# Output projections in split float32r by column halves with loads behind each half, and the first expert's rows selected from X by TensorE

## The reference, cut to what matters

```python
h = mixer_ab(x, ...)                 # layer 0: retention heads and pooling; mixed @ w_out at its end
h = mixer_c(x, ...)                  # layer 1: sparse attention; o @ w_out at its end
x = layer_norm(ALPHA * x + h, ln1_g[i], ln1_b[i])
m = hierarchical_moe(x, ...)         # top group, top 2 of its 8 experts; each expert:
                                     #   a, b = split(xt[tok] @ w_gu[e]); (silu(a) * b) @ w_down[e]
x = layer_norm(ALPHA * x + m, ln2_g[i], ln2_b[i])
x = x + sigmoid(x @ ple_w_gate[i]) * (p[i] @ ple_w_proj[i])
```

## Time and profile before

| | us |
|---|---|
| median of 3 runs | 1652.06 (1650.83 to 1652.81) |
| the profiled execution | 1653.78 |
| its span, first to last instruction | 1651.9 |
| mean granted TensorE clock | 0.957 |

### The profile page before, as it was taken

One profiled execution on the slowest core, in us unless ns is written; L12 is line 12 of the kernel. 1 busy time (PEld: TensorE's weight loads), 2 busy tenths in 40 slices (PEclk: granted clock), 3 DMA queues, 4 the chain that ended last, 5 costly groups with the idle time before them and its releaser, 6 DMA issues. The chain is left out here.

```text
span 1651.9 us, 17175 instructions
## 1 busy us (share of the span) xinstructions
PE 1441.9 (87%) x6216; PEld 684.8 (41%) x6216; DVE 410.2 (25%) x1020; ACT 314.9 (19%) x642; POOL 207.5 (13%) x327
## 2 busy tenths in 40 slices
PE   6998998998887789879998988989987888889887
PEld 5885463332222233224444456853322323333243
DVE  3424351000000001044068354330000000101172
ACT  3212011111011101012234574111101101101121
POOL 0000001211111111100000253011211111111100
PEclk9999989999999999999999999979999999999989
DMA  7107358999999999994200003299999999999840
GB/s 284 51 26 267 139 193 335 411 426 429 430 429 428 430 429 428 424 371 170 109 1 1 1 2 115 83 426 424 427 431 428 429 429 429 428 429 428 358 171 38
DMA packets 78306, 482.57 MB, mean 292 GB/s; under 512 B 18400, under 2 KB 20452, under 8 KB 45480
## 3 DMA queue, kind: packets, MB, share of 16 engines
q1 hardware_dynamic: 65800, 463.76, 67.5%
q0 software_dynamic: 10240, 16.82, 2.7%
q10 hardware_dynamic: 2208, 1.20, 0.2%
HBM read 474.91 MB, written 23.59 MB: 302 GB/s over the span
## 5 line engine op out<-in xcount | busy, mean ns | idle before, releaser
L910 PE MATMUL PS<-wide,w 128*64 128x512 f32 x1984 | 448.3, 601 | 49.4 <-ACT w L929 29.0
L924 PE MATMUL PS<-slim,w 128*64 128x512 f32 x992 | 252.8, 655 | 78.4 <-issue 77.0
L910 PEld LDWEIGHTS PS<-wide,w 128*64 128x64 f32 x1984 | 136.4, 138 | 329.4 <-issue 255.2
L924 PEld LDWEIGHTS PS<-slim,w 128*64 128x64 f32 x992 | 84.2, 149 | 241.2 <-issue 239.1
L936 DVE TENSOR_TENSOR w<-w,PS 128x256 f32<-128x256 f32 x64 | 27.0, 422 | 543.8 <-ACT w L933 543.8
L933 ACT ACTIVATE w<-PS 128x256 f32<-128x256 f32 x64 | 24.5, 383 | 501.8 <-PE PS L910 501.8
L1174 PE MATMUL PS<-wide,XT 128*128 128x512 f32 x256 | 117.8, 617 | 2.3 <-ACT XT L176 2.3
L1485 ACT ACTIVATE w<-PS,w 128x512 f32<-128x512 f32 x62 | 42.6, 687 | 313.2 <-PE PS L924 313.2
L939 DVE COPY w<-PS 128x256 f32<-128x256 f32 x64 | 27.2, 425 | 297.9 <-PE PS L917 297.9
L1352 POOL COPY w<-w 128x1 uint32 (+1 forms) x62 | 11.2, 181 | 660.3 <-ACT w L1485 660.3
L883 POOL DMA_INDIRECT w<-x_rows,w x64 | 67.2, 1050 | 72.3 <-POOL w L1345 51.6
(11 more groups left out here) (232 smaller groups left out, 1627.8 us busy)
## 6 DMA issues: line engine op xcount, KB each, us to landing
wide<-in_moe_w_gu SPq DMA_DIRECT2D x124, 2048.0 KB, 25.8
slim<-in_moe_w_down SPq DMA_DIRECT2D x62, 2048.0 KB, 25.7
w<-in_moe_w_gu SPq DMA_DIRECT2D x4, 2048.0 KB, 12.2
wide<-in_ple_w_gate SPq DMA_DIRECT2D x4, 2048.0 KB, 14.2
w<-in_ab_w_in SPq DMA_DIRECT2D x2, 2048.0 KB, 14.0
w_in<-in_ab_w_in SPq DMA_DIRECT2D x2, 2048.0 KB, 7.5
x_rows<-X SPq DMA_DIRECT2D x8, 512.0 KB, 2.6
XT<-in_moe_w_down SPq DMA_DIRECT2D x2, 2048.0 KB, 29.1
```

Source lines behind the costliest of these rows:

```text
L910: m = pe.matmul(PS[u * SLOTS:(u + 1) * SLOTS, 2 + q, :], xeT[q][:, k, :], gu[k].rearrange("p (a u c) -> p a u c", a=2, u=2)[:, :, u, :], s ...
L924: m = pe.matmul(PS[u * SLOTS:(u + 1) * SLOTS, 6 + q, :], gT[:, k, :], dn[k][:, u * NB:(u + 1) * NB], start=(k == 0), stop=(k == FF // P - 1))
```

## The change

1. Layer 0's output weights and mix are split too, and its 64 float32 products become 192 in float32r. The weights' raw halves are loaded during the input projection, once its sixteenth job is done. The first half is split there by ACT and DVE, the second in the retention stage by ACT and POOL. For each row of the mix ACT writes MT_HIGH and MT_RAW from bank 7 and POOL subtracts; for the last row DVE does it from PSUM.
2. `out_projection` goes over the column halves outside and the tiles inside, in both layers; layer 1's output weights are laid out by halves.
3. SP's loads stand in three places: before the sums (`load_first`), after the first column half (`load_half_way`), and after the last sum (`load_after_products`), this one ahead of the last tile's store to x_rows. In layer 0, expert 0 isn't loaded in the retention stage any more.
4. Expert 0's rows aren't gathered: DVE makes a selection matrix FIRST from the ranks, and TensorE multiplies X with it (`place_first`), before GP. The gather of expert 1 is alone. The filler products after GP are gone.

The diff, cut to its core:

```diff
+            OUT_RAW = [three(again(f"out_raw{c}", of, 0, 4096, F32)[:, :], NB) for c, of in enumerate(("w_high1", "w_low1"))]
+            OUT_LOW = [three(again(f"out_low{c}", of, 0, 4096)[:, :], NB) for c, of in enumerate(("w_high1", "w_low1"))]
+            OUT_HIGH = [three(again(f"out_high{c}", of, 0, 4096)[:, :], NB) for c, of in enumerate(("w_in0", "x_high"))]
+            MT_RAW = three(again("mixed0_raw", "w_low0", 0, 4096, F32)[:, :], SEQ)
+            MT_LOW = three(again("mixed0_low", "w_low0", 0, 4096)[:, :], SEQ)
+            MT_HIGH = three(again("mixed0_high", "x_low", 0, 4096)[:, :], SEQ)
...
+                    pj.wait_full(sp, 15)
+                    for c in range(2):
+                        sp.dma_start(OUT_RAW[c], rows(A["ab_w_out"][0, :, c * NB:(c + 1) * NB], NB))\
+                          .then_inc(s_wout[c], 16)
...
+                        if j in (16, 17):
+                            act.wait_ge(s_wl, len(PIECES))
+                            act.wait_ge(s_wout[0], 16)
+                            for k in range(4 * (j - 16), 4 * (j - 15)):
+                                act.activation(OUT_HIGH[0][:, k, :], OUT_RAW[0][:, k, :], ACT.Copy).then_inc(s_oh, 1)
...
+                    for k in range(KD):
+                        dve.wait_ge(s_oh, k + 1)
+                        dve.tensor_tensor(OUT_LOW[0][:, k, :], OUT_RAW[0][:, k, :], OUT_HIGH[0][:, k, :].bitcast(F32),
+                                          ALU.subtract).then_inc(s_ol, 1)
+                    dve.wait_ge(s_ol, KD)
...
-                sp.dma_start(w_out0[0], rows(A["ab_w_out"][0, :, 0:NB], NB)).then_inc(s_wout[0], 16)
-                sp.dma_start(w_out0[1], rows(A["ab_w_out"][0, :, NB:D], NB)).then_inc(s_wout[1], 16)
-                load_gu(sp, 0, 0, 0)
-                load_dn(sp, 0, 0, 0)
...
+                j = len(LAST) - 1
+                k = row_of(j)
+                dve.wait_ge(s_mh, j + 1)
+                dve.scalar_tensor_tensor(MT_LOW[:, k, :], PS[:, 7, :], gains[:, k:k + 1], MT_HIGH[:, k, :].bitcast(F32),
+                                         ALU.mult, ALU.subtract).then_inc(mt.sem_of(j), 1)
+                mt.wait_emptied(dve, j)
...
+            def _(pool):
+                for k in range(KD):
+                    pool.wait_ge(s_oh1, k + 1)
+                    pool.tensor_tensor(OUT_LOW[1][:, k, :], OUT_RAW[1][:, k, :], OUT_HIGH[1][:, k, :].bitcast(F32),
+                                       ALU.subtract).then_inc(s_ol1, 1)
+                for j in range(len(LAST) - 1):
+                    k = row_of(j)
+                    mt.wait_emptied(pool, j)
+                    pool.tensor_tensor(MT_LOW[:, k, :], MT_RAW[:, k, :], MT_HIGH[:, k, :].bitcast(F32), ALU.subtract)\
+                        .then_inc(s_ml, 1)
...
+                act.wait_ge(s_wout[1], 16)
+                for k in range(KD):
+                    act.activation(OUT_HIGH[1][:, k, :], OUT_RAW[1][:, k, :], ACT.Copy).then_inc(s_oh1, 1)
                 for j, (kind, i) in enumerate(LAST):
                     mt.wait_full(act, j)
-                    k = i if kind == "turn" else 4 + i
-                    act.activation(MT[:, k, :], PS[:, 7, :], ACT.Copy, scale=gains[:, k:k + 1])\
-                       .then_inc(mt.sem_of(j), 1)
...
-                    for t in range(T):
-                        for c in range(2):
+                    for c in range(2):
+                        for t in range(T):
                             pairs = products(t, c)
                             for r, (lhsT, rhs) in enumerate(pairs):
                                 m = pe.matmul(PS[:, 2 * t + c, :], lhsT, rhs, start=(r == 0),
                                               stop=(r == len(pairs) - 1))
                             m.then_inc(sums.full, 1)
-                            if t >= 2 and c == 0:
+                            if c == 1 and t >= 2:
                                 if t == 2:
                                     pe.wait_ge(s_wr, 64)
                                 logits(t - 2)
-                        if t >= 1:
-                            pe.wait_ge(norm.done, t)
-                            turn.pe(pe, t - 1)
+                            if c == 1 and t >= 1:
+                                pe.wait_ge(norm.done, t)
+                                turn.pe(pe, t - 1)
...
+                    for c in range(2):
+                        for t in range(T):
+                            sums.wait_full(dve, c * T + t)
                             xs = X[:, t, c * NB:(c + 1) * NB]
                             dve.scalar_tensor_tensor(xs, xs, ALPHA, PS[:, 2 * t + c, :], ALU.mult, ALU.add)\
                                .then_inc(sums.sem_of(0), 1)
-                            sums.wait_emptied(dve, 2 * t + c)
+                            sums.wait_emptied(dve, c * T + t)
                             norm.dve_stats(dve, own, t, c)
-                        norm.dve_tile(dve, own, t)
+                            if c == 1:
+                                norm.dve_tile(dve, own, t)
...
+                    sums.wait_full(sp, T - 1)
+                    load_half_way(sp)
                     for t in range(T):
+                        if t == T - 1:
+                            sums.wait_full(sp, 2 * T - 1)
+                            load_after_products(sp)
                         sp.wait_ge(norm.done, t + 1)
                         sp.dma_start(x_rows[t * P:(t + 1) * P, :], X[:, t, :]).then_inc(s_rows, 16)
                     load_ln(sp, A["ln2_g"][l], A["ln2_b"][l], s_ln)
-                    then_load(sp, sums)
+                    load_dn(sp, l, 1, 1)
...
-                for q in range(2):
-                    gather(pool, q, R["taken"][:, q:q + 1], s_gath[q])
+                gather(pool, 1, R["taken"][:, 1:2], s_gath[1])
...
+                dve.wait_ge(s_values, 1)
+                own.done(dve.tensor_tensor(FIRST_TWO, RS[:, :, 0:SLOTS], over_columns(OH[:, :, 0], SLOTS), ALU.mult))
+                dve.tensor_tensor(FIRST, FIRST_TWO[:, 0:T, :], FIRST_TWO[:, T:2 * T, :], ALU.add).then_inc(s_first, 1)
...
-                        pe.wait_ge(s_gath[q], 16 * i + 16)
+                        pe.wait_ge(s_gath[q], 16 * i + 16 * q)
                         turn_gathered(pe, q).then_inc(s_turn[q], 1)
+
+                    def place_first():
+                        for c in range(4):
+                            for u in range(2):
+                                xs = X[:, :, u * NB:(u + 1) * NB].rearrange("p t (f c) -> p t c f", c=4)
+                                for t in range(T):
+                                    m = pe.matmul(PS[:, 0, c * P + u * SLOTS:c * P + (u + 1) * SLOTS], xs[:, t, c, :],
+                                                  FIRST[:, t, :], start=(t == 0), stop=(t == T - 1))
+                        m.then_inc(s_turn[0], 1)
...
+                    pe.wait_ge(s_first, 1)
+                    place_first()
                     pe.wait_ge(s_listed, 1)
                     for u in range(2 * T):
                         m = pe.matmul(GP, RS[:, u, :], GATES[:, u, :], start=(u == 0), stop=(u == 2 * T - 1))
                     m.then_inc(s_gates, 1)
-                    keep_running(pe, 12, 5)
...
-                    turn(0, 0)
...
-                    sp.dma_start(three(wide[0][:, :], D), rows(A["c_w_out"][0], D)).then_inc(s_cwout, 16)
+                    for c in range(2):
+                        sp.dma_start(three(wide[0][:, c * 4096:(c + 1) * 4096], NB),
+                                     rows(A["c_w_out"][0, :, c * NB:(c + 1) * NB], NB)).then_inc(s_cwout, 16)
...
-        def before_out(l):
-            def load_first(sp):
-                load_third_gu(sp, l)
-            return load_first
-
-        def after_out(l):
-            def then_load(sp, sums):
-                sums.wait_full(sp, 7)
-                if l == 1:
-                    load_gu(sp, 1, 0, 0)
-                    load_dn(sp, 1, 0, 0)
-                load_gu(sp, l, 1, 1)
-                load_dn(sp, l, 1, 1)
-            return then_load
+        def load_first_0(sp):
+            load_third_gu(sp, 0)
+            load_gu(sp, 0, 1, 1, halves=(1,))
+
+        def load_half_way_0(sp):
+            load_gu(sp, 0, 0, 0, halves=(0,))
+            load_gu(sp, 0, 1, 1, halves=(0,))
+
+        def load_after_products_0(sp):
+            load_gu(sp, 0, 0, 0, halves=(1,))
+            load_dn(sp, 0, 0, 0)
+
+        def load_first_1(sp):
+            load_third_gu(sp, 1)
+
+        def load_half_way_1(sp):
+            load_gu(sp, 1, 0, 0, halves=(1,))
+            load_gu(sp, 1, 1, 1, halves=(0,))
+
+        def load_after_products_1(sp):
+            load_gu(sp, 1, 0, 0, halves=(0,))
+            load_dn(sp, 1, 0, 0)
+            load_gu(sp, 1, 1, 1, halves=(1,))
...
         def first_products(t, c):
-            return [(MT[:, k, t * P:(t + 1) * P], w_out0[c][:, k, :]) for k in range(KD)]
```

(21 more changed lines are left out.)

52 lines of the change are left out of this document (31 added, 21 removed).

## The result

| | before | after |
|---|---|---|
| median, us | 1652.43 | 1670.74 (1668.11 to 1671.77, 4 runs) |
| ratio | | 1.0107, 95% interval 1.0091 to 1.0123 |
| profiled execution, us | 1653.78 | 1668.11 |
| mean granted TensorE clock | 0.957 | 0.946 |

The change makes the kernel 1.1% slower; 0.5% faster was forecast. The medians differ by 18.3 us, the two profiled executions by 14.3: the profiled one after the change is the fastest of its four. First the page of the changed kernel, which answers to the earlier trace rows: part 1 and the slices of the DMA engines.

The account below looks back on a forecast made before the run. The prediction took the expert loop as bound by DMA loads, its beginning in layer 0 by the first expert's start. Terms of -7.15 us (layer 0) and -1.0 (layer 1), together -8.2, gave a 1643.9 us median; 8 in 10 within 1633 to 1651.

Parts of the forecast that it names:

- B to X0: Start of routing to expert 0's first product: placement replaces the gather's latency; +0.85 us in layer 0, -0.8 in layer 1.
- rival B: Clock stays at half through place_first (14.5 us, not 8.5) and the first expert: 15.7 us more, 1659.6 us; chance 0.09.
- the first expert's products take 7.1 us: First expert's products: TensorE comes without a pause, 7.1 us instead of 8.55 and 9.39; -1.45 and -2.3 us.
- the sum of -8.2: All steps of both layers together: -7.15 us in layer 0 and -1.0 in layer 1.
- Retention, +3.1: Layer 0's retention stage, before the projection's products: second ACT copies and DVE's last subtraction add 3.1 us, bounds 1.6 and 5.5.
- Rival C: POOL and DVE block each other in the retention stage: 5.1 us more, 1649.0 us; chance 0.12.
- Products of layer 0, -12.6: Layer 0's output projection: 192 float32r products replace float32 ones, 50.6 us instead of 63.2, so -12.6.
- Products of layer 1, -1.9: Layer 1's output projection: same product count, only tile 1's logits move behind the last product; -1.9 us.
- E to B, +2.95 and +7.8: Projection's last product to start of routing: store to x_rows waits behind queued loads; +2.95 us layer 0, +7.8 layer 1.
- Rival A: Store to x_rows isn't held up by the loads: 2.95 and 7.8 us more gained, 1633.1 us; chance 0.17.
- Length of the expert stage, -3.8 in layer 1: First expert's products to the loads behind the experts: earlier loads bring layer 1 to layer 0's 453.0 us, -3.8.
- T: Theory for a_gather: place_first is the loss, so undoing it gains some 16 us against the changed kernel, 1654.

Follow-up runs that it names:

- d_contig: Changed kernel with place_first's weights read as 128 adjacent words of X instead of every fourth, features landing in wrong places; 1657.8 us, ratio 1.0046.
- g_f32: Changed kernel with FIRST as weights, last store ahead of the loads, and one float32 product of high parts in layer 0's projection instead of three; 1646.3 us.
- c_store: Changed kernel with SP's loads after the last sum issued behind the last store to x_rows, not ahead of it; 1659.4 us, ratio 1.0036.
- a_gather: Changed kernel with part 4 alone undone: expert 0's rows gathered from x_rows and transposed again, filler products back; 1643.3 us, ratio 0.9938.
- b_swap: Kernel before with part 4 alone, but FIRST as the weights and X moving; 1650.2 us, ratio 0.9976.
- e_swap: Changed kernel with place_first's operands exchanged: FIRST as weights, X moving in 512 adjacent words, result copied and transposed; 1641.6 us, ratio 0.9929.
- f_mid: Changed kernel with FIRST as weights, X moving, and one 2 MB load ahead of the last store, the other loads behind it; 1632.5 us, ratio 0.9883.
- i_fill: Changed kernel with two filler products of ident behind each four products of the placement; 1685.5 us, ratio 1.0190.

## Why the prediction was wrong, point by point

**The failed step** is the cost of `place_first` in "B to X0": "The nearest rows are the logits, 16 records in 1.87 us at full clock and 3.63 at half: 7.5 or 14.5 us. I take 8.5". Number and shape of the records were right, and the rows of the logits were rows of adjacent weights. `place_first` reads X as `(f c)` with c = 4, so its weight loads step over four words. That was in the diff and not in the price. Measured: 15.2 us, some 0.235 a record, above even the 14.5 of rival B, which was taken from the clock alone. The rows with the same step in the kernel before, the transposes of gathered tiles, would have misled too: 0.121 us from start to start at full clock. Only d_contig beside the change shows the price. d_contig gives 7.36 us for the same records at full clock with adjacent weights, so the price by the logits was right for what it stood for.

**The second part of the same step** is the clock. The argument was that GP's and MP's rows just before are at full speed and TensorE then has no pause. The stretches show the clock falling 2 us into `place_first` nonetheless, and the gate products and the first expert behind it pay. "the first expert's products take 7.1 us" became 8.96 and 9.60. Rival B named this mechanism, with a chance of 0.09, and half the right reason. That its price of 14.5 us is near the measured 15.2 is luck: the records start 0.233 us apart at either level of the clock. Its 1659.6 us is 11 short of the 1670.7; 3.2 of them are the gate products, which it left at full clock (3.57 us measured, 2.0 in the sum). Put in at their measured sizes, place_first (2 x 6.7), the gate products (2 x 1.6) and the first experts (1.9 and 2.5) add 21.0 to the sum of -8.2: +12.8, where the profiled executions show +14.3 and the medians +18.3. The rest are small steps of either sign, the products and the experts of layer 1 above all.

**Retention, +3.1:** the chain is right, the exact hit is luck. The first product of the projection comes 3.1 us later, but the retention stage began 0.65 us sooner, and it is 3.8 us longer (from 130.00 and not 130.65 to the first product). The transposes of the heads came 0.7, 1.4, 2.2 and 2.3 us later within the stage, as reckoned; the last ones then ran at half clock (1.09 us, 0.63 before), which the sum didn't have. Rival C was there in part. The multiplications of DVE took, beside POOL's subtractions:

```profile
147.56 1.27 POOL L587 TENSOR_TENSOR mixed_low<-mixed_raw,mixed_high 128x512 fp32r<-128x512 f32 x1 [1.87 <-ACT mixed_raw L605]
147.83 1.54 DVE L570 TENSOR_TENSOR wide<-wide,w 128x512 f32<-128x512 f32 x1
...
158.99 0.69 DVE L570 TENSOR_TENSOR wide<-wide,w 128x512 f32<-128x512 f32 x1
```

Two of four, which began within a subtraction, took 1.54 and 1.64 us and ended some 0.5 after it; the two that didn't took 0.69. By the rule of the Trainium skill ("SBUF — State Buffer", section "SBUF: two separate sides") the later of the two blocks wholly, and the trace agrees. It came to 1.8 us of DVE's time in all, not to 5.1, and to no delay of TensorE: its transposes came no later than ACT's second copies make them.

**Products of layer 0, -12.6:** right, -13.3 in the traces. g_f32 gives 11.4 for the split alone; the logits of tile 1, which part 2 moves behind the last product (1.87 us), are the rest.

**Products of layer 1, -1.9:** -0.4. The logits did move, but the first sum ran at half clock for 3 us (0.57 from 1015 to 1019 us), where in the kernel before it ran at 1.00 from 1013 to 1017. In g_f32, with the same products in layer 1 and the clock at 1.00 there, they took 47.2 us in place of 49.1: the -1.9 is right where the clock stays. Why it fell is open.

**E to B, +2.95 and +7.8:** right, +3.6 and +8.3, by the mechanism named; the store landed 9.2 us after its issue in layer 0 and 13.9 in layer 1, and c_store takes the wait away. Rival A is excluded.

**B to X0, the gather:** "the gather's latency is exchanged for products of the same length" would hold for adjacent weights at full clock. a_gather shows also that the thing given up had become cheaper by the change itself: 18.2 us from B to X0 in layer 1 in place of 21.7. The prediction took the gather's cost from a trace in which loads ran beside it.

**Length of the expert stage, -3.8 in layer 1:** right in kind, -2.4. b_swap agrees with the reason given: in the kernel before, an earlier X0 brought layer 1 nothing.

**What the sum gives without part 4:** -6.55 in layer 0 and +2.1 in layer 1 (the terms up to B and the length of the expert stage), -4.45 together. a_gather measured -10.1. The difference stands at the first experts: their products took 7.09 us in both layers, in place of 8.55 and 9.39, and in layer 1 they began 3.5 us sooner after B, 7.2 us in all, of which smaller steps take some back. Both are gains that came with the clock (1.00 through these products) and the gather's faster landing, and that the prediction had put down to the placement or left out. Against the change, the same 7.09 stands in place of 8.96 and 9.60, and X0 comes 8.9 and 10.3 us sooner after B: 23.5 of the 27 us, where T had 16.

## What to carry to other kernels

Price a weight load by its access pattern as well as by its count, and from rows of the same kind of instruction: a float32 product's record with a step of four words cost 0.235 us here and one with adjacent words 0.115, while transposes with the same step took 0.121. Where a product needs a stepped selection of a large tensor, try it with the small tensor as the weights, the large one moving in adjacent words, and the turning afterwards: e_swap did the same work in 5.35 us (3.65 at full clock) and 1.5 us of copy and transposes. Before a DMA on the critical path is replaced, ask what it costs once the rest of the change is in: by then the gather was worth 2 us, not the 7 that its landing took before. And on one queue, put at most as much in front of a store that somebody waits for as still lets it land before the other engines are done: one load of 2 MB, issued 5.4 us ahead, was free in f_mid, two and three cost 3.6 and 8.3 us in the change.

## What the runs showed of the hardware that was not expected

A record of these products with stepped weights takes the same time at both levels of the clock: in i_fill eight took 2.08 us at a granted clock of 1.00 and 1.95 at 0.50. With adjacent weights it is 0.115 and 0.21. A transpose with the same step takes 0.121 at full clock.
The granted clock fell to 0.50 after the start of the placement's 64 records, without any gap in them: 1.8 and 3.1 us after it in the change, 0.7 us in layer 0 of d_contig, while it stayed at 1.00 through them in layer 1. With fillers between them it fell too. With e_swap's 16 records of 512 columns it fell as well, 0.7 us after their start in layer 0, but what followed was at full clock again. What decides it these runs don't show.
The two gathers took 7.0 and 8.9 us to land beside the loads and 3.0 and 2.8 without them.
